# A two-layer hybrid encoder on one core: start-up loads in k order, gate sums by scans, norm sums in PSUM, score copies moved

## The reference

```python
for l in range(2):
    h = rmsnorm(x, g_mix[l]); p = h @ w_in[l]                 # 1024 -> 3104 columns
    u, va, q, k, vb, g, r_f, r_b = split(p)                   # r_f, r_b: 16 columns each
    out_a = gelu(u) * (w_s[head] @ layernorm(gelu(va)) + b_s) # 4 heads, chunks of 128 tokens
    la_f = log_sigmoid(r_f @ w_gate_f + b_gate_f) / 16        # decay of the forward scan, 256 wide
    la_b = log_sigmoid(r_b @ w_gate_b + b_gate_b) / 16
    # per chunk: cum = cumsum(la); scores = (q*exp(cum)) @ (k*exp(-cum)).T, masked;
    # states from k*exp(cum_last - cum); the backward direction with the time reversed
    o = gla(q, k, vb, la_f) + gla_reversed(q, k, vb, la_b)
    out_b = rmsnorm(o, g_gla) * silu(g)
    x = x + concat(out_a, out_b) @ w_out[l]
    h = rmsnorm(x, g_ffn[l])
    z = dwconv3(h @ w_up[l]); x = x + (silu(z_gate) * z_val) @ w_down[l]   # 1024 -> 5632, 2816 -> 1024
return rmsnorm(x, g_final)
```

## Time and profile before

| | before |
|---|---|
| median of three runs | 1150.17 us |
| the profiled execution: time | 1148.53 us |
| its span, first to last instruction | 1146.7 us |
| PE busy | 1122.5 us (98%) |
| DVE, ACT, POOL busy | 547.2, 482.8, 465.7 us |
| mean granted clock of PE | 0.994 |

### The profile page before, as it was taken

The page is one execution under the profiler, slowest core; times in us unless marked ns, Lnnn a source line. Parts: engine busy times, 40 slices in busy tenths (PEclk is TensorE's granted clock), DMA queues, the critical chain, the costliest instruction groups (busy, mean ns, idle before and its releaser), DMA issues.

```text
span 1146.7 us, 16739 instructions
## 1 busy us (share of the span) xinstructions
PE 1122.5 (98%) x5302; PEld 928.1 (81%) x5302; DVE 547.2 (48%) x796; ACT 482.8 (42%) x649; POOL 465.7 (41%) x199
## 2 busy tenths in 40 slices
PE   7999999999999999999999999999999999999997
PEld 6788888788888888888878878787888888888885
DVE  6334685665414552155633257856552255413554
ACT  5654343564314542244547343445542354313441
POOL 3333233354454444444632432344444444354450
PEclk8999999999999999999999999999999999999999
DMA  7222112232232232232422221222323232232221
GB/s 286 74 84 82 57 58 90 74 110 96 88 110 92 94 108 93 91 107 96 147 98 74 74 80 52 72 92 93 110 91 111 75 108 91 92 109 92 92 73 74
DMA packets 31681, 108.65 MB, mean 95 GB/s; under 512 B 3722, under 2 KB 3850, under 8 KB 31628
## 3 DMA queue, kind: packets, MB, share of 16 engines
q1 hardware_dynamic: 30396, 105.85, 27.3%
q10 hardware_dynamic: 1232, 2.12, 0.5%
HBM read 105.85 MB, written 2.10 MB: 94 GB/s over the span
## 4 chain that ended last, share of the span: by engine, by line
PE 90%; DVE 5%; ACT 2%; issue 2%; DMA 1%; ACTq 0%; DVEq 0%
PE acc L878 25%; PE acc L879 24%; PE acc L880 24%; PE acc L994 3%; PE acc L996 3%; PE acc L995 3%; DVE xg_lo L557 1%; DVE ssq L564 1%; ACT xg_hi L288 1%; DVE x L794 1%; PE side L1047 1%; DMA x<-xT 1%; PE acc L948 1%; PE side L1083 1%; PE side L965 1%
## 5 line engine op out<-in xcount | busy, mean ns | idle before, releaser
L270 POOL TENSOR_TENSOR w_lo<-w_raw,w_hi 128x1024 fp32r<-128x1024 f32 x192 | 465.1, 2426 | 653.8 <-ACT w_hi L279 653.8
L878 PE MATMUL acc<-xg_hi,w_hi 128*128 128x512 f32 x864 | 340.7, 394 | 0.8 <-DVE xg_lo L557 0.8
L880 PE MATMUL acc<-xg_hi,w_lo 128*128 128x512 f32 x864 | 336.4, 389 | 0.0
L879 PE MATMUL acc<-xg_lo,w_hi 128*128 128x512 f32 x864 | 336.3, 389 | 0.0
L279 ACT ACTIVATE w_hi<-w_raw 128x1024 fp32r<-128x1024 f32 x192 | 201.6, 1055 | 254.5 <-PE acc L880 210.0
L878 PEld LDWEIGHTS acc<-xg_hi,w_hi 128*128 128x128 f32 x864 | 162.2, 188 | 36.2 <-DVE xg_lo L557 1.6
L880 PEld LDWEIGHTS acc<-xg_hi,w_lo 128*128 128x128 f32 x864 | 162.2, 188 | 33.9
L879 PEld LDWEIGHTS acc<-xg_lo,w_hi 128*128 128x128 f32 x864 | 162.3, 188 | 33.4 <-issue 1.0
L878 PE MATMUL acc<-feat_hi,w_hi 128*128 128x512 f32 x480 | 187.0, 390 | 2.4 <-DVE feat_lo L735 2.4
L831 DVE SCALAR_TENSOR_TENSOR arena<-side,conv_sb,arena 128x511 f32<-128x511 f32 x176 | 132.0, 750 | 117.8 <-ACT arena L506 105.0
L879 PE MATMUL acc<-feat_lo,w_hi 128*128 128x512 f32 x480 | 186.8, 389 | 0.0
(11 more groups left out here) (130 smaller groups left out, 869.5 us busy)
## 6 DMA issues: line engine op xcount, KB each, us to landing
w_raw<-slabs SPq DMA_DIRECT2D x192, 512.0 KB, 3.3
x<-xT ACTq DMA_DIRECT2D x4, 512.0 KB, 9.4
outT<-arena SPq DMA_DIRECT2D x8, 256.0 KB, 2.2
ln_sb<-ln_gb SPq DMA_DIRECT2D x2, 512.0 KB
spatial_sb<-spatial_w SPq DMA_DIRECT2D x2, 256.0 KB
spatial_b_sb<-spatial_b SPq DMA_DIRECT2D x2, 256.0 KB
gate_sb<-gate_w SPq DMA_DIRECT2D x2, 130.0 KB
rank_raw<-rank_w SPq DMA_DIRECT2D x1, 256.0 KB, 10.5
```

Of the source, the lines that this page charges most:

```text
L270: pool.tensor_tensor(w_lo[:, w], w_raw[:, w], w_hi[:, w].bitcast(F32), ALU.subtract).then_inc(lo_done, 1)
L878: pe.matmul(out, wh, ah, start=first, stop=False)
L879: pe.matmul(out, wh, al, start=False, stop=False)
L880: return pe.matmul(out, wl, ah, start=False, stop=last)
```

## The change

The start: x arrives in six pieces (`X_GROUPS`) and slabs 0 and 1 in three parts each (`W_PARTS`: 256, 256 and 512 columns, that is blocks 0-1, 2-3, 4-7); SP and ACT issue them in turns in the order of k; ACT and POOL split the parts as they come, and PE takes x tiles in groups (0, 1), (2, 3), (4, 5), (6), (7), both slabs at each tile. Slabs 2 and 3 come behind all of x and are split later; POOL takes their low parts only when all eight `xg_lo` tiles are done. `keep_busy` runs 16 products instead of 24. On PE four short branches are new (waits that hold in the second layer only).

The gates: `z` is formed with channels on partitions, 64 rows of ranks (kept in two copies, rows 0 to 63 and 64 to 127) per product, even and odd channel tiles on opposite halves of the rows. The bias moves to ACT's Abs and to a new DVE instruction, min(z + b, 0), in place in PSUM. The sum over a chunk's tokens is a DVE scan, four per tile and 16 in a layer, in place in PSUM, the backward ones with reversed step; the 16 triangle products go. ACT's exponentials stand ahead of the split of slab 9.

The norm sums: `ssq_part` is a PSUM bank; the first square is copied there, the next ones added in place, and the last sum is written to SBUF. The memsets of `ssq` and the loops around the two places are gone. The scores: ACT copies and DVE selects heads 0 and 1 ahead of the layer norm's root, and heads 2 and 3 together.

The diff, cut to its core:

```diff
+PAIRED |= {f"z{t}": (t + 3) % RING for t in range(4)}
-def encoder(nc, xT, slabs, rank_w, gate_w, spatial_w, spatial_b, ln_gb, gains, gla_gain, conv, consts, outT):
+X_GROUPS = ((0,), (1,), (2,), (3,), (4, 5), (6, 7))
+W_PARTS = (slice(0, 2 * P), slice(2 * P, 4 * P), slice(4 * P, SLAB))
...
-        rank_split = sb("rank_split", [P, 2 * RW + P - 4 * RANK], F32R)
-        gate_sb = sb("gate_sb", [4 * RANK + 1, 4 * P])
+        rank_split = sb("rank_split", [P, KT * P], F32R)
+        gate_sb = sb("gate_sb", [P, 4 * P])
+        gate_b_sb = sb("gate_b_sb", [P, DEPTH * 4])
...
+        ssq_part = side_banks[2][:, :]
...
+            load_part(0, 0)
+            load_part(1, 0)
+            load_x(sp, 1)
+            load_part(0, 1)
+            load_part(1, 1)
+            load_x(sp, 3)
+            load_part(0, 2)
+            load_part(1, 2)
+            load_x(sp, 5)
+            sp.dma_start(rank_raw[:, 0:DEPTH * RW], rank_w).then_inc(rank_loaded, 16)
+            load_slab(0, 0, 2)
+            load_slab(0, 0, 3)
...
+            for j, part in ((0, 0), (1, 0), (0, 1), (1, 1), (0, 2), (1, 2)):
+                w = slice(j * SLAB + W_PARTS[part].start, j * SLAB + W_PARTS[part].stop)
+                if part < 2:
+                    pool.wait_ge(hi_part[j], part + 1)
+                else:
+                    pool.wait_ge(hi_done, j + 1)
+                pool.tensor_tensor(w_lo[:, w], w_raw[:, w], w_hi[:, w].bitcast(F32),
+                                   ALU.subtract).then_inc(lo_part[j] if part < 2 else lo_done, 1)
+            pool.wait_ge(xg_ready, KT)
+            for j in (2, 3):
+                w = slice(j * SLAB, (j + 1) * SLAB)
+                pool.wait_ge(hi_done, j + 1)
...
-            load_and_split(0)
-            load_and_split(1)
+            first_gain(0)
+            split_part(0, 0)
+            split_part(1, 0)
+            first_gain(1)
+            first_gain(2)
+            split_part(0, 1)
+            split_part(1, 1)
+            first_gain(3)
             square(0, 0, 0)
             square(1, 0, 1)
-            load_and_split(2)
-            load_and_split(3)
+            first_gain(4)
+            split_part(0, 2)
+            split_part(1, 2)
+            square(2, 0, 2)
+            square(3, 0, 3)
+            first_gain(5)
             act.wait_ge(rank_loaded, 16)
             rank_hi(0)
-            for m in range(2, KT):
-                square(m, 0, m)
+            square(4, 0, 4)
+            square(5, 0, 5)
+            act.wait_ge(raw_loaded[2], 16)
+            split_hi(2)
+            square(6, 0, 6)
+            square(7, 0, 7)
+            act.wait_ge(raw_loaded[3], 16)
+            split_hi(3)
...
-                for t in range(CH):
-                    side_wait(f"z{t}")
-                    act.activation(softplus[t], side(f"z{t}")[:, :], ACT.Abs).then_inc(softplus_done, 1)
+                act.wait_ge(vec_loaded, 4 * 16)
+                for t in range(4):
+                    act.wait_ge(z_ready[t % 2], L * 2 + (t // 2 + 1))
+                    act.activation(softplus[t], side(f"z{t}")[:, :], ACT.Abs,
+                                   bias=gate_b_sb[:, bass.ds(L * 4 + t, 1)]).then_inc(softplus_done, 1)
...
                 copy_score(0)
+                copy_score(1)
                 act.wait_ge(mv_done, L * 16 + 16)
...
-                copy_score(1)
                 copy_score(2)
+                copy_score(3)
                 gelu_u(1)
                 acc_at(N_U + 3)
                 split_after(L, 14)
-                copy_score(3)
...
             def add_square(m, r, buffer):
+
                 dve.wait_ge(sq_done, r * KT + m + 1)
-                dve.wait_ge(ssq_added, r * (KT + 1) + m + 1)
-                dve.tensor_tensor(ssq[:, :], ssq[:, :], sq[buffer], ALU.add).then_inc(ssq_added, 1)
+                if m == 0:
+                    dve.tensor_copy(ssq_part, sq[buffer]).then_inc(ssq_added, 1)
+                else:
+                    dve.wait_ge(ssq_added, r * KT + m)
+                    dve.tensor_tensor(ssq_part if m < KT - 1 else ssq[:, :], ssq_part, sq[buffer],
+                                      ALU.add).then_inc(ssq_added, 1)
...
+            gain_lo(4, 0)
+            gain_lo(5, 0)
+            add_square(2, 0, 2)
+            add_square(3, 0, 3)
+            gain_lo(6, 0)
+            gain_lo(7, 0)
+            rank_lo(0)
...
+                    z_t = side(f"z{t}")[:, :]
+                    dve.wait_ge(softplus_done, L * 12 + (2 * t + 1))
+                    dve.tensor_scalar(z_t, z_t, gate_b_sb[:, bass.ds(L * 4 + t, 1)], 0.0, ALU.add,
+                                      ALU.min).then_inc(negative_done, 1)
+                for t in range(4):
                     dve.wait_ge(softplus_done, L * 12 + (8 + t + 1))
-                    dve.scalar_tensor_tensor(out=la[t], in0=side(f"z{t}")[:, :], scalar=0.0, in1=softplus[t],
-                                             op0=ALU.min, op1=ALU.subtract).then_inc(la_done, 1)
+                    dve.wait_ge(negative_done, L * 4 + (t + 1))
+                    for c in range(CH):
+                        first, last = c * P, (c + 1) * P - 1
+                        w = slice(first, last + 1) if t < 2 else slice(last, first - 1 if c else None, -1)
+                        dve.tensor_tensor_scan(side(f"z{t}")[:, w], side(f"z{t}")[:, w], softplus[t][:, w], 0.0,
+                                               ALU.add, ALU.subtract).then_inc(cum_done, 1)
...
-                for tiles in ((0, 1, 2, 3), (4, 5), (6,), (7,)):
-                    for j in range(2):
-                        if tiles[0] == 0:
-                            pe.wait_ge(hi_done, L * NS + (j + 1))
-                            pe.wait_ge(x_done, L * NX + (j + 1))
-                        for k in tiles:
+                for tiles in ((0, 1), (2, 3), (4, 5), (6,), (7,)):
+                    part = min(tiles[0] // 2, 2)
+                    for k in tiles:
+                        for j in range(2):
+                            if k == 0:
+                                pe.wait_ge(x_done, L * NX + (j + 1))
+                            if k == 0:
+                                pe.wait_ge(hi_part[j], 1)
+                                with pe.If(L > 0):
+                                    pe.wait_ge(hi_done, L * NS + (j + 1))
+                            if k == 2:
+                                pe.wait_ge(hi_part[j], 2)
+                            if k == 4:
+                                pe.wait_ge(hi_done, L * NS + (j + 1))
...
-                for t in range(CH):
-                    pe.matmul(side(f"z{t}")[:, :], rankT[:, t * P:(t + 1) * P], gate_sb[:, :],
-                              start=True, stop=True).then_inc(side_ready, 1)
+                for t in range(4):
+                    a = (t % 2) * DK
+                    pe.matmul(side(f"z{t}")[:, :], gate_sb[a:a + DK, t * P:(t + 1) * P], rankT[a:a + DK, :],
+                              start=True, stop=True).then_inc(z_ready[t % 2], 1)
...
-                for dt in range(4):
-                    pe.wait_ge(la_done, L * 4 + 4)
-                    for c in range(CH):
-                        last = pe.matmul(side(f"cum{dt}")[:, c * P:(c + 1) * P], la[c][:, dt * P:(dt + 1) * P],
-                                         upto if dt < 2 else since, start=True, stop=True)
-                    last.then_inc(side_ready, 1)
```

More of the change, by code:

```diff
@@ L49 @@
 assert NS % RING == 0 and N_FFN % RING == 0 and N_LAST % RING == 0 and LAST_TILES % 2 == 0
-SIDE = (["rankT", "spread", "sum"] + [f"z{t}" for t in range(4)] + [f"cum{t}" for t in range(4)]
+SIDE = (["rankT", "spread", "sum"]
         + [f"keys{c}" for c in range(4)] + [f"state{s}" for s in range(3)]
@@ L116, in encoder @@
         o_rstd_parts = sb("o_rstd_parts", [P, 2 * 16], F32R)
-        ident, upto, since, after = (consts_sb[:, i * P:(i + 1) * P] for i in range(4))
+        ident, after = (consts_sb[:, i * P:(i + 1) * P] for i in range(2))
         def slot(i, n=1):
@@ L124, in encoder @@
         A = [slot(h) for h in range(4)]
-        la = [slot(4 + t) for t in range(4)]
-        keT = la
+        keT = [slot(4 + t) for t in range(4)]
         kend = [slot(c) for c in range(4)]
-        osq = la
+        osq = keT
         softplus = [slot(12 + t) for t in range(4)]
@@ L232, in load_slab, with load_part @@
                              ).then_inc(raw_loaded[j], 16)
+            def load_part(j, part):
+                w = W_PARTS[part]
+                sp.dma_start(w_raw[:, j * SLAB + w.start:j * SLAB + w.stop],
+                             slabs[j:j + 1, :, w].rearrange("o p n -> (o p) n")
+                             ).then_inc(raw_part[j][part] if part < 2 else raw_loaded[j], 16)
+            load_part(0, 0)
[10 more added lines that the diff above has]
+            load_slab(0, 0, 3)
             with sp.Fori(0, DEPTH) as L:
-                for j in range(RING):
-                    load_slab(L, 0, j)
```

(23 more changed lines are left out.)

118 lines of the change are left out of this document (60 added, 58 removed).

## The result

The changed kernel takes 1122.6 us (median of 4 runs, 1122.26 to 1122.98) beside 1148.59 us for the kernel before (1146.97 to 1150.57): a ratio of 0.9773, 95% interval 0.976 to 0.9786. I had forecast 1127.0, 1120 to 1134. The gain is 26.0 us where the sum had 22.4.

What follows compares the result with a forecast made beforehand. PE, busy 98% of the span, was taken to bound the kernel. Terms 8.2 + 7.1 + 2.7 + 3.6 + 1.1 - 0.3 = 22.4 us gave 1126.1 or 1127.8; forecast 1127.0, range 1120 to 1134.

Steps and rivals of the forecast that it cites:

- 1. The start: Program start: new load and split order brings the rank products from 29.5 to 21.3 us, gain 8.2 (3 to 11.9).
- the forecast's own chance of three in four: Program start: no half clock on PE; the opposite case, one in four, was charged at 2 us.
- DMA does not bind: Program start: 3.1 MB of x and two slabs at 387 GB/s arrive by 11 us, so loads set no limit.
- 2. The triangle products: Gate stage: 16 PE products a layer go, replaced by hidden DVE scans of 0.4 us; gain 7.1 us over both layers.
- 3. the gate products: Gate stage: 64-row products run two at a time, 2.1 us instead of 3.44 a layer; gain 2.7 us (ends 0 to 3.4).
- rival (d): Gate stage: scans slow enough that PE waits for the keys, so the kernel gets slower, 1160 us at 2.0 a scan; chance 0.03.
- 4. The scores: Second score pair: PE's wait for ACT's copy of head 1's scores goes; gain 1.8 us a layer, 3.6 in all.
- 5. The norm sums elsewhere: Out-projections: shorter DVE sums end PE's wait for the last `xg_lo`, gain 1.1 us; down-projections 0.
- the branches: Four new branches on PE, run in layer 1: cost 0.3 us (0 to 2.2).
- (a): Program start gives only half: PE starved, half clock returns, slab pair ends at 25.5, gain 4, total 1131 us; chance 0.15.
- (b): Mixing stretch: time saved returns as PE's wait for `feat_lo` at the out-projection, gain only 16.1, total 1133 us; chance 0.12.
- (c): Program start reaches PE's own work limit without half clock, whole gain 26.1, total 1123 us; chance 0.10.

Runs made afterwards that it cites:

- The square: Four kernels with new gates and scores: old start order with norm sums in SBUF 1133.23 us, in PSUM 1125.23; new order in SBUF 1137.84, in PSUM 1122.6.
- the two kernels on the old gates: The kernel before, unchanged (1148.59 us), and the kernel before with only its running norm sums moved to PSUM (1138.38 us).
- The old gate stage: The changed kernel with 65-row gate products, sums into `la` and triangle products put back and no scans: 1132.77 us.

## Why the prediction was right, and where it was off

**1. The start, 8.2 forecast, 9.4 measured.** The events came as laid out: rank products at 19.99 (20 to 22), the last `xg_lo` ended at 17.7 (18 to 19), no half clock, PE within reach of its tiles all along. It was the forecast's own chance of three in four, and its charge for the fourth, 0.5 us, is part of the difference. What was off is what the gain was put down to. The step said "the new order, engine by engine" and took the sums in PSUM along as four times 0.69. The square and the two kernels on the old gates show 5.4 to 6.0 us from the sums alone, at the gate products, in the old order, and the order on top of them 3.6; without them the order costs 1.7. So the number held, but not the reason that stood first. The held row of two sums at 12.38 us (3.68) was in the trace of before, directly ahead of the row at 15.98 in the earlier trace rows, and I did not price it. "DMA does not bind" was too strong as well: ACT stood 0.9 us for a slab part at 9.23, and with SP's loads in another order the rank products come 3.4 us later (23.41).

**2. The triangle products, 7.1, and 3. the gate products, 2.7: 9.8 forecast, 10.0 measured.** The old gate stage returned exactly that. A scan took 0.32 us where I took 0.4. The last key product ended at 57.2 and the transposes came at 65.7; laid out were 56.9 and 65.9 (24 and 33 behind the gate products). So 8.5 us of cover are left and rival (d) never came near. With 3.57 for the triangle products, 1.4 of the 5.0 a layer are left for the gate products, against 1.35. The pairing was real: on one half of the rows they cost 1.75 a layer more, above the 1.4 because 64 rows that don't pair are 0.3 dearer, from start to start, than the 65 before.

**4. The scores, 3.6 forecast, 3.6 measured**: 9.45 us from pair to pair became 7.65 in both layers, and undoing it brought the wait back.

**5. The norm sums elsewhere, 1.1, and the branches, -0.3: 0.8 forecast, 3.8 measured. The step that failed.** The out-projections gave 0.65 each, near the 0.55 of the forecast, and the branches cost 0.4. But "at the down-projections PE doesn't wait for them: 0" is wrong. From the feed-forward spread of the first layer to the rank products of the second:

| | sums in SBUF | sums in PSUM |
|---|---|---|
| kernel before, and its sums alone changed | 369.41 | 366.40 |
| old order, new gates and scores | 370.29 | 366.32 |
| changed kernel | 370.14 | 366.93 |

3.0 to 4.0 us, in three pairs. I had read the 2.16 us without a named wait in the earlier trace rows as the price of the jump alone. The loss is a longer gap (2.2 to 3.2 us) and, behind the gap, a stretch at 0.43 us a matmul; the kernels with sums in PSUM have gaps of 0.7 to 1.2 us and no such stretch. In the first pair that is all: 1.4 us of gap and eight products 0.2 dearer make 3.0. One thing is common to all fourteen traces: the first product of the second layer comes 2.7 to 3.4 us behind the start of a 16 KB transfer on the queue for instructions. In the window from 553 to 556 us of the changed kernel, and in that from 566 to 569 of the kernel with the sum in SBUF, it reads:

```profile
q8 instruction: 1, 0.02, 1.8%
```

```profile
q8 instruction: 1, 0.02, 1.9%
```

With sums in PSUM it starts 1.5 to 1.9 us ahead of the start of the old layer's last product (ten traces), with sums in SBUF between 0.2 ahead and 0.8 behind it (four). That fits a fetch of the loop's first code, hidden behind the work in hand or not. The kernel before with its busy products written out supports it: DVE and POOL stand as before, the transfer starts 1.1 us later relative to the last product (0.8 behind instead of 0.2 ahead), and the gap is 1.0 longer. In two kernels with sums in SBUF the profile puts the gap down to DVE's `x` (the 2.9 above), but that sum had ended 0.9 us before the product in one and 1.0 in the other. Why TensorE asks for the code later when the sums are in SBUF stays open.

**The rivals.** (a) Half the start: no; even the old order with sums in PSUM has its pair of slabs done at 23.6, not at 25.5. (b) A later wait: `feat_lo` stayed at 1.2 a layer. (c) The floor, 1123: by its time this came nearest, for 1122.6 lies inside 1120 to 1134 but below the forecast's own 1123.5 to 1130.5. It didn't by its mechanism: the start stopped at 19.99 and not at 17.6, and the 2.5 us at the border, not foreseen, made up for it. That the time lies so near to (c) is luck. By spans the gain is 26.2, 3.8 above the sum: 1.2 at the start, 3.0 in the fifth term with the branches and 0.2 at the gates, less 0.6 behind the last spread. One slip in the sum: the upper ends of its terms add up to 27.6 (11.9 + 7.1 + 3.4 + 3.6 + 1.6), not 29, so the 1120 at the end of the range had no term behind it.

## What to carry to other kernels

When DVE adds a running sum whose operands all lie in SBUF and POOL works on SBUF at the same time, look at the row of each sum and at what stands behind it in DVE's order: up to 2.1 us a sum were lost here (2.8 against 0.69), and accumulating in a free PSUM bank was worth 8 to 15 us. Test two edits of one stretch in all four combinations before pricing either: the new order of loads costs 2.3 us or more with one home of the sum and gives 2.3 with the other. An idle time without a named wait at a loop's jump is not a fixed price: compare where the instruction transfer starts, and whether a half clock follows.

## What the hardware showed that I had not expected

The copy of a square into PSUM isn't held by POOL. The same copy in the same place of the old order, once into PSUM and once into SBUF, each with a low part of POOL (2.80 and 2.83 us, from 11.73 and 11.75) across it:

```profile
12.20 0.69 DVE L586 COPY side<-arena 128x512 f32<-128x512 f32 x1
```

```profile
12.23 2.63 DVE L586 COPY ssq<-arena 128x512 f32<-128x512 f32 x1
```

The forecast had left open whether the one copy might be held; it isn't, and undisturbed the copy within SBUF takes 0.42 us. The Trainium skill (SBUF — State Buffer, on who interferes with whom) says that a copy can enter a two-port mode, and can then contend with GpSimd, when its operands meet conditions that another of its pages gives. Here the copy within SBUF was held and the one into PSUM was not.

Four sums in a row that meet POOL's low parts take turns with them, 2.8 us for each, instead of one being held once. And the half clock's price depends on where it falls, though each matmul takes 0.43 us instead of 0.23 either way: from 11.9 to 15 us, with the last tile ready only at 21.57, it moved the rank products by 0.5 us at most; from 21.7 us on, with the last tile ready at 22.95, its whole price was lost, 2.8 us by 27.4.
